# Branch stages of a hybrid decoder step: head norms, pooling, gathers and sample slots rearranged

## What is computed

```python
def _layer(x, ...):
    z = _rmsnorm(x, g1) @ w_in      # q k v | pooling input | mLSTM q k v, gates, output gate | 3 branch gates
    q, k = head-wise _rmsnorm(q), _rmsnorm(k)
    ya = sliding-window attention, window 128, 8 heads of 64, relative bias, sink per head
    yb = (trailing mean over 2/4/8/16 tokens, on four groups of 128 channels, minus the token) @ w_pool * pool_scale
    h  = mLSTM in chunks of 128 tokens (4 heads of 128), state C, n, m carried from chunk to chunk
    yc = head-wise _rmsnorm(h) * sigmoid(co)
    x  = x + (sigmoid(ga)*(ya@w_a) + sigmoid(gb)*(yb@w_b) + sigmoid(gc)*(yc@w_c)) @ w_out
    return x + _peer(_rmsnorm(x, g2))

def _peer(x):                       # for each token, 8 heads
    q = x @ wq; s1, s2 = q's halves @ 128 keys each
    top 16 of s1, top 16 of s2, top 16 of the 256 sums -> 16 experts of 16384, gates = softmax
    act = gelu(x . u[expert])
    y   = sum over 8*16 experts of gate * act * v[expert]
```

## Time and profile before

| | |
|---|---|
| median of 3 runs | 3914.45 us (3912.28 to 3915.92) |
| profiled execution | 3923.08 us, span 3921.3 us |
| TensorE matmul busy | 3242.6 us (83%) |
| VectorE busy | 2233.8 us (57%) |
| ScalarE busy | 1116.5 us (28%) |
| GpSimd busy | 1256.5 us (32%) |
| granted TensorE clock | 0.920 of 2.4 GHz over the span |
| DMA | 1317.12 MB, 336 GB/s; gathers 1082.20 MB |

### The profile page before, as it was taken

The page is one execution under the profiler, slowest core; times in us unless marked ns, Lnnn a source line. Parts: engine busy times, 40 slices in busy tenths (PEclk is TensorE's granted clock), DMA queues, the critical chain, the costliest instruction groups (busy, mean ns, idle before and its releaser), DMA issues. The chain is left out here.

```text
span 3921.3 us, 32232 instructions
## 1 busy us (share of the span) xinstructions
PE 3242.6 (83%) x10262; PEld 1874.4 (48%) x10262; DVE 2233.8 (57%) x5139; ACT 1116.5 (28%) x3364; POOL 1256.5 (32%) x1148
## 2 busy tenths in 40 slices
PE   7788879879989799669979799674699898778777
PEld 4577544446656444346656444342366563332222
DVE  0421577674556767664648665473545487764444
ACT  1211233342223323432223322342212233332222
POOL 0100233333433344343334333341233234443342
PEclk9789889989999899789999899886899999997999
DMA  5134899789999999679999898587899799999998
GB/s 161 58 100 144 331 366 395 292 329 363 420 397 389 378 408 421 244 297 415 420 392 406 350 353 334 220 339 231 318 373 389 264 404 411 421 420 265 421 421 372
DMA packets 204992, 1317.12 MB, mean 336 GB/s; under 512 B 23320, under 2 KB 27464, under 8 KB 72175
## 3 DMA queue, kind: packets, MB, share of 16 engines
q0 software_dynamic: 148736, 1082.20, 69.3%
q1 hardware_dynamic: 52631, 220.29, 15.0%
q10 hardware_dynamic: 3456, 12.58, 0.8%
HBM read 1298.67 MB, written 17.64 MB: 336 GB/s over the span
## 5 line engine op out<-in xcount | busy, mean ns | idle before, releaser
L1859 POOL DMA_INDIRECT arena<-uv,eidx x1040 | 1175.4, 1130 | 2358.8 <-PE ps L876 1797.1
L876 PE MATMUL ps<-arena,dgs 128*128 128x512 f32 x3508 | 1668.8, 620 | 255.1 <-ACT dgs L1178 253.8
L1410 DVE CUSTOM_DVE_ANT_0 arena<-arena,xx 128x1024 f32<-128x1024 f32 x1024 | 1236.9, 1224 | 695.9 <-DMA arena<-uv,eidx 671.4
L876 PEld LDWEIGHTS ps<-arena,dgs 128*128 128x128 f32 x3508 | 670.9, 198 | 1089.5 <-issue 698.6
L1159 ACT ACTIVATE gel<-dots 128x2 f32<-128x2 f32 (+1 forms) x520 | 105.0, 202 | 1643.4 <-DVE dots L1410 1642.3
L909 PE MATMUL ps<-wbuf,xT 128*128 128x420 f32 (+1 forms) x1152 | 428.2, 522 | 8.9 <-DMA wbuf<-w_z 7.7
L1057 PE MATMUL ps<-xT,wbuf 128*128 128x256 f32 (+1 forms) x1536 | 357.9, 387 | 5.8 <-DMA wbuf<-w_merge 3.7
L1057 PEld LDWEIGHTS ps<-xT,wbuf 128*128 128x128 f32 x1536 | 295.7, 193 | 75.1 <-issue 19.4
L1178 ACT ACTIVATE dgs<-cst,wgt 128x128 f32<-128x128 f32 x877 | 312.3, 395 | 16.7
L909 PEld LDWEIGHTS ps<-wbuf,xT 128*128 128x128 f32 (+1 forms) x1152 | 205.2, 180 | 232.0 <-issue 222.0
L1630 DVE SCALAR_TENSOR_TENSOR T<-T,ps 128x256 f32<-128x256 f32 (+1 forms) x96 | 40.6, 423 | 412.2 <-PE ps L1061 412.2
(11 more groups left out here) (353 smaller groups left out, 2087.6 us busy)
## 6 DMA issues: line engine op xcount, KB each, us to landing
wbuf<-w_merge SPq DMA_DIRECT2D x96, 768.0 KB, 8.5
wbuf<-w_z SPq DMA_DIRECT2D x64, 840.0 KB, 8.2
wbuf<-w_q SPq DMA_DIRECT2D x64, 512.0 KB, 8.0
arena<-uv,eidx POOLq DMA_INDIRECT x1040, 11.6
wbuf<-w_o SPq DMA_DIRECT2D x32, 512.0 KB, 7.8
xin<-x_prompt SPq DMA_DIRECT2D x8, 1024.0 KB, 8.5
grow<-gains SPq DMA_DIRECT2D x8, 512.0 KB, 9.5
xin<-biasfull SPq DMA_DIRECT2D x4, 1024.0 KB, 4.7
```

The lines of the kernel that those rows point to most:

```text
L876: done = mm(ps[:, half, :], dgs[:, j, :], ring[:, j, row_], start=(q == 0), stop=(q == P - 1), skip_group_check=True)
L1410: v.tensor_tensor_reduce(ring[0:rows_, j, 0:D], ring[0:rows_, j, 0:D], x, 1.0, 0.0, ALU.mult, ALU.add, dots[0:rows_, j:j + 1]).then_inc(s[ ...
L1859: g.indirect_dma_start(ring[0:rows_, j, :], None, uv, bass.IndirectOffsetOnAxis(ap=experts, axis=0)).then_inc(got[j], 16)
```

## The change

- **Head norms.** `head_norms` and `head_scales` run on VectorE in the projection, at chunks 5 and 11; ScalarE's square root, exponential and logarithm at chunk 8, the output gate's sigmoid at chunk 13. ScalarE's copies of q, k and of the pooling and mLSTM inputs are gone; the transposes read `z`.
- **Pooling** is a product with a band matrix on TensorE (four of 128x128 a tile, four of 16 columns for the rows of the tile before), copied by ScalarE to `pooled`. `pinT`, `tab` and `pool_tile` are gone; the table of constants that stays on the chip grows from 592 to 1168 columns.
- **GpSimd** issues gathers only, with no bound but the free ring buffers. The keys are shifted by VectorE; values and pooling rows of the tile before are read from `z` or, once a pass, from a copy by ScalarE.
- **Attention.** VectorE divides the softmax numerators before they are transposed, in two halves; the product with V is four matmuls of 512 columns, and gives the transposed result directly.
- **Norm of h**: squares, sums and the products with gate and gain are taken per tile, the rest jointly at the end.
- **Slots on VectorE.** In the last projection residues 1, 3, 5, 7 in place of 3: 171 slots in all.
- **Sample loads.** `sample_early` issues the stores and small loads in the branches of the last pass, behind `L0_ready` of its second tile; keys and values are loaded straight from the caches, only the last row of the keys from k_s. VectorE's order in the sample stage changes: mLSTM gates first, q and k norm after, pooling last.
- **Sample slots**: 8 of 128 rows (SPK = 8, slots 896 to 903). Experts 8 to 15 of each head are copied to partitions 64 to 127.
- **Start.** x is loaded before the constants; the spread of the bias table waits nowhere ahead of the first weights, and the bias load stands at weight chunk 8.
- VectorE ends a tile's sum one point later; the second weight load of a merge no longer waits for the pooling.

```diff
-SLOTS = TILES * P + PK
+SPK = PK // 2
+SLOTS = TILES * P + SPK
-ON_VECTOR = {"z": (3,), "b": (1, 5), "m": (1, 4, 6), "o": (1, 3, 5), "f": (2,)}
+ON_VECTOR = {"z": (3,), (LAST, "z"): (1, 3, 5, 7), "b": (1, 5), "m": (1, 4, 6), "o": (1, 3, 5), "f": (2,)}
...
@@ SyncE, the last pass
+        def sample_early(sp, at):
+            sp.dma_start(scr_qk, zs_scr[:, CQ0:CQ0 + 1024]...); sp.dma_start(scr_g..., zs_scr[:, G0:G0 + 8]...)
+            sp.dma_start(k_s[:, 0:W - 1, :], cache_k[:, 1:W, :]); ... v_s, pool_s likewise, selT, sel
+            sp.wait_ge(s["c_scr"], 32)
+            sp.wait_ge(s["tile_v"], tile.at("L0_ready", TILES))
+            g32, q32, k32, n32, c1, misc, relrep, sbuck loaded
         def sample_loads(sp, at):
             sp.dma_start(zs, zs_scr)
             sp.dma_start(spool[0:NS * HIST, :], state_pool...)
+            sp.dma_start(Ks[0:W - 1, :, :], cache_k[:, 1:W, :]...)
             load_c(0)
+            load_qk(0)
+            sp.dma_start(Vs[0:W - 1, :, :], cache_v[:, 1:W, :]...); sp.dma_start(Vs[W - 1:W, :, :], zs_scr[:, V0:V0 + P]...)
-            sp.wait_ge(s["kscr"], 64)
-            sp.dma_start(Ks, k_s.rearrange("n k c -> k n c")).then_inc(s["k_load"], 16)
-            sp.dma_start(Vs, v_s.rearrange("n k c -> k n c")).then_inc(s["k_load"], 16)
+            sp.dma_start(Ks[W - 1:W, :, :], k_s[:, W - 1:W, :]...)
...
@@ TensorE, branches
-                    pe.wait_ge(s["qks_ready"], here)
+                    pe.wait_ge(s["qkn"], p + 1)
-                        tr(ps[:, 2, j * P:(j + 1) * P], qks[:, j * P:(j + 1) * P], ident)
+                        tr(ps[:, 2, j * P:(j + 1) * P], z[:, t, j * P:(j + 1) * P], ident)
-                    for j in range(4):
-                        last = tr(ps[:, 6, j * P:(j + 1) * P], pcs[:, j * P:(j + 1) * P], ident)
+                    for c in range(4):
+                            mm(ps[:, 6, cols_], own, band[:, c, :], start=True, stop=False, skip_group_check=True)
+                            last = mm(ps[:, 6, c * P:c * P + 16], rows_, prev_band[64:P, c, :], start=False, stop=True, ...)
-                    pe.wait_ge(s["P_exp"], here)
                     for half in range(2):
+                        pe.wait_ge(s["P_normed" if half else "Pa_normed"], here)
-                    for h in range(AH):
-                        mm(ps[:, 2, o:o + AD], PT[:, 2 * h, :], vprev[:, 64 * kv:64 * kv + 64], start=True, stop=False)
-                        last = mm(ps[:, 2, o:o + AD], PT[:, 2 * h + 1, :], z[:, t, V0 + 64 * kv:...], start=False, stop=True)
+                    for kv in range(AKV):
+                        mm(out, z[:, 0, V0...] if t else vprev[...], PT[:, heads, :][:, 0::2, :], start=True, stop=False)
+                        last = mm(out, z[:, t, V0...], PT[:, heads, :][:, 1::2, :], start=False, stop=True)
-                    for j in range(4):
-                        last = tr(ps[:, 2, j * P:(j + 1) * P], qks[:, j * P:(j + 1) * P], ident)
-                    last.then_inc(s["yaT_tr"], 1)
...
@@ VectorE, projection and branches
+                    if c == 5:
+                        head_norms(p)
+                    if c == 11:
+                        head_scales(p)
+                    v.tensor_copy(kTr[:, 0:P], kTr[:, P:2 * P]).then_inc(s["tile_v"], tile.step("k_moved"))
+                    v.tensor_tensor(L[:, 0:AG, :], L[:, 0:AG, :], arden[:, 0:AG]..., ALU.mult).then_inc(s["Pa_normed"], 1)
+                    v.tensor_tensor(L[:, AG:AH, :], L[:, AG:AH, :], arden[:, AG:AH]..., ALU.mult).then_inc(s["P_normed"], 1)
...
@@ GpSimd
-            for p in range(PASSES):
-                for t in range(NT):
-                    ahead(p, "b", t, 0)
-                    pool_tile(p, t)
-                    ahead(p, "b", t, 3)
-                    shift_keys(p, t)
-                    ahead(p, "b", t, 6)
-                    shift_values(p, t)
             gather(SLOTS)
```

More of the change, by code:

```diff
@@ L609, in sample_vector @@
             v.scalar_tensor_tensor(n32, n32, c1[:, 19:20], t32, ALU.mult, ALU.add).then_inc(s["smp_v"], SMP["v"].step("c_nn2"))
+            point(LAST, "x", 1)
+            dve.wait_ge(s["r40"], n)
+            zq = zs[:, 0:640].rearrange("p (h d) -> p h d", d=AD)
+            v.tensor_tensor(zq, zq, r40[0:NS, 0:10].unsqueeze(2).broadcast_to([NS, 10, AD]), ALU.mult).then_inc(s["smp_v"], SMP["v"].step("q_qk_scaled"))
+            dve.wait_ge(s["smp_v"], SMP["v"].at("q_qk_scaled"))
+            v.tensor_tensor(zs[:, 0:640], zs[:, 0:640], row[0:NS, R_QK:R_QK + 640], ALU.mult).then_inc(s["qkn"], 1)
+            point(LAST, "x", 2)
+            dve.wait_ge(s["smp_a"], SMP["a"].at("b_T"))
+            for c, w in enumerate(POOLW):
+                last = v.tensor_reduce(psum_s[:, c, :], full[:, c, :, 16 - w:16], AX.X, ALU.add)
+            last.then_inc(s["smp_v"], SMP["v"].step("b_s1"))
+            dve.wait_ge(s["smp_v"], SMP["v"].at("b_s1"))
+            for c, w in enumerate(POOLW):
+                last = v.scalar_tensor_tensor(pool_s_in[:, c, :], psum_s[:, c, :], 1.0 / w, full[:, c, :, HIST], ALU.mult, ALU.subtract)
+            last.then_inc(s["smp_v"], SMP["v"].step("b_p"))
+            point(LAST, "x", 3)
             dve.wait_ge(s["smp_p"], SMP["p"].at("a_qtr"))
@@ L754, in _, with weights @@
             used = [None]
-            def weights(src, shape, count, sem, base, per, between=(), free_after=None):
+            def weights(src, shape, count, sem, base, per, between=(), later=None):
                 width = int(np.prod(shape))
@@ L771, in weights @@
                 for i in range(2, count):
+                    if i == 8 and later:
+                        later()
                     sp.wait_ge(sem, base + per * (i - 1))
@@ L828, in _ @@
                 tiles = len(tiles_of(p))
-                weights(w_z, (HALF, ZP), NZ, s["z_mm"], NZ * tiles_before(p), tiles, [lambda: load_bias(p)])
+                weights(w_z, (HALF, ZP), NZ, s["z_mm"], NZ * tiles_before(p), tiles, [lambda: load_bias(p)] if p else [spread_bias], None if p else lambda: load_bias(p))
                 if p == LAST:
@@ L877, in add_slots @@
                         else:
-                            done = mm(ps[0:NS, 4 + half, :], dgs[0:PH * NS, j, 0:NS], ring[0:PH * NS, j, row_],
-                                      start=(q == 0), stop=(q == PK - 1), skip_group_check=True)
+                            done = mm(ps[0:NS, 4 + half, :], dgs[:, j, 0:NS], ring[:, j, row_],
+                                      start=(q == 0), stop=(q == SPK - 1), skip_group_check=True)
                     done.then_inc(free[j], 1)
@@ L1398, in point @@
                 first, last = PLAN[p].get(key, (0, 0))
+                if first == last:
+                    return
+                if ended[0] < TILES - 1 and passed[0] > last_of(ended[0]):
+                    end_tile(ended[0])
+                passed[0] = first
                 for n in range(first, last):
@@ L1415, in point @@
                         unadded.append(n)
-                if ended[0] < TILES - 1 and first > last_of(ended[0]):
-                    end_tile(ended[0])
             def norm(p, which):
@@ L1906 @@
         C[bucket[W - 1 - i], C_SBUCK + i] = 1.0
[L1907 to L1911 removed]
+    selmat = np.zeros((P, NS + P), f)
+    for i in range(P):
+        selmat[i, i % NS] = 1.0
+        selmat[i % NS, NS + i] = 1.0
     perm = np.array([kv * AG + j for j in range(AG) for kv in range(AKV)])
```

459 lines of the change are left out of this document (214 added, 245 removed).

## The result

The changed kernel takes 3828.15 us (median of 4 runs, 3815.5 to 3835.04) against 3913.36 before: ratio 0.9778, 95% interval 0.9757 to 0.9799. It is faster, by 85 us in the medians and by 97.7 in the profiled executions (3825.35 us against 3923.08), and outside my range, which ended at 3820.

The account below looks back on a forecast made before the run. No engine was full: the branches were taken as a chain of short steps, DMA as the floor where slots run freely. Terms -5 + 4 - 88 - 28 - 27 - 36 = -180 from 3923.08, scaled by 0.9978, gave 3735 us; 8-in-10 range 3660 to 3820.

Parts of the forecast that it names:

- Sample loads early and without the round trip of keys and values: Sample stage: TensorE's 19.5 us wait goes, and some two thirds of an 11.7 us load wait; -27 us.
- Head norms: Head of the branches: TensorE's 47.2 us wait before the first transpose goes, -47; table loads in projections 1 and 2, +4.
- Pooling from GpSimd: Branches: gathers no longer queue behind GpSimd's pooling; 15 us in each of passes 2 and 3, 4 in pass 1, -34.
- Softmax normalised before the transposes: Branches: second normalisation lies on the chain, transposes of the attention output go; +0.4 us a tile, +3 in all.
- h norms per tile: End of the branches: squares of both tiles leave the path to ycT; -2.5 us a pass, -10.
- Projection 3: Last projection: 24 more slots on VectorE shorten the stage from 237.9 to 210 us; -28, bounds -41 to -12.
- Sample slots of 128 rows: Tail: half the instructions for the same bytes; the 36 us of DMA time lost in a 90 us hole go, -36.
- The smaller sum beside it: Tail: if 64-row gathers were not narrow and only TensorE was late, 40 - 27 = 13 us instead of 36.
- Rival B: Branches held by ring buffers TensorE frees late and dots in order, so the stall is not GpSimd's; 3823 us, chance 0.19.
- the 20 to 40 that I gave as a sign of being right: Branches 2 and 3: dots' waits for gathers at 20 to 40 us in place of 52 and 48.
- C, the pace of DMA: Branches fall to DMA's pace, 121 us against 179.5 and 179.8; 3648 us, chance 0.19.
- D: Merges and projections: weights land late as gathers share the DMA engines, so the kernel is slower; 4051 us, chance 0.05.

Follow-up runs that it names:

- Experiment 12: Changed kernel with 127-row loads cut into 112 and 15 and the branches' end reordered, head norms, gates and sigmoid back at the head of the branches: 3799.18 us, ratio 0.9702.
- experiment 4: Kernel before the change without GpSimd's ten pooling operations and its wait for the transposed pooling input, pooled part left out: 3883.79 us, ratio 0.9917.
- experiment 6: Changed kernel with 127-row loads cut into 112 and 15, almost all of the pooling's band products left out: 3765.4 us, ratio 0.9612.
- experiment 7: Changed kernel with 127-row loads cut into 112 and 15, without the two products that divide the softmax numerators: 3771.31 us, ratio 0.9623.
- experiment 5: Changed kernel with 127-row loads cut into 112 and 15, joint h norm and yc copy moved before the last point's dots: 3760.3 us, ratio 0.9603.
- experiment 10: Changed kernel with 127-row loads cut, branches' end reordered, pooling products moved, plus per-tile h norm behind the copy of the softmax transposes' second half: 3745.09 us, ratio 0.9565.
- experiment 3: Changed kernel with 127-row loads cut into 112 and 15, last projection's VectorE slots back to one residue of 8 in place of four: 3823.44 us.
- experiments 1 and 2: Changed kernel with 127-row key and value loads cut into 112 and 15: 3790.1 us; with the round trip back, 128-row loads from k_s and v_s: 3788.41 us.
- experiment 8: Changed kernel with 127-row loads cut into 112 and 15, the tail's last 120 slots gathering only 64 of 128 rows: 3794.2 us, ratio 0.968.

## Why the prediction was wrong

The direction was right and most steps too; the step that failed is *Sample loads early and without the round trip of keys and values*, and behind it two costs put at nothing or almost.

- *Head norms* (-47 and +4): right. Experiment 12 has 39 us for the 43.
- *Pooling from GpSimd*: the -34 was right in size (30 by experiment 4), its working only in part: the dots' waits for gathers fell by 12 us in branches 2 and 3, not by 30, and the slower operations of VectorE, which the sum had at nothing, are in the 30 too. "On TensorE four products of 128x128 a tile come in for four transposes and half a softmax transposition that leave: nothing" was wrong: the products cost 25 us (experiment 6), less what the transposes had cost. I had left out the four of 16 columns beside them, each with a weight load of its own, and I took TensorE's idle share for room. The net of the pooling's move is some 5 us and what the transposes had cost.
- *Softmax normalised before the transposes* (+3): 19 to 22 (experiment 7), less what left with the old division. I had one of two scalings beside other work; here both cost about their length.
- *h norms per tile* (-10): the joint part stayed behind six dots and two row adds, TensorE's wait grew from 6.1 to 11.3 us, and 30 us were left lying (experiment 5), 14 more in the order of the per-tile part, probably (experiment 10).
- *Projection 3* (-28): -40 in the profile, 33 in the medians (experiment 3). VectorE's row adds did not hold up the dots as I had feared (VectorE is busy 168.66 us); the bound of 194 from DMA was nearly reached, 197.7.
- *Sample loads* (-27): the step that failed, +33 for the stage. With the loads cut the stage and branches 3 are 31 us shorter than before, the stage alone some 14. The wait of 19.5 us that I let go with the round trip did not go: TensorE waits 21.6 us without the round trip and 20.9 with it (experiments 1 and 2). The number of rows was in the diff, 127 in place of 128, and I priced the loads by bytes and by the trip that went.
- *Sample slots of 128 rows* (-36): right, -33, and by the cause weighed there, not by TensorE alone (experiment 8). The 32 matmuls last 20 us at 421 GB/s, and the hole is gone. The smaller sum beside it, 40 - 27 = 13, set twelve of the sixteen slots against all eight; the sixteen took 48 us, which makes it 21.

Rival B named 3823 us, near what came, but not for its reason: the pooling on GpSimd cost 30 us (experiment 4) and projection 3's gain stayed (experiment 3). Its picture of the branches was half right: the dots still wait for gathers, 42.0 and 38.4 us in branches 2 and 3 of the changed kernel, at the upper end of the 20 to 40 that I gave as a sign of being right. C, the pace of DMA, needs branches of 121 us; 164 came, and 140 with fewer slots. D did not happen: weights land in 8.4 us, and TensorE's waits for them are no longer than before:

```profile
wbuf<-w_merge SPq DMA_DIRECT2D x96, 768.0 KB, 8.4
```

By the experiments' sizes the forecast's -180 becomes about -180 + 38 (loads) + 25 (pooling products) + 16 (scaling) - 7 (projection 3) + 4 (pooling on GpSimd) + 4 (heads) + 3 (tail) = -97, against -97.7. That it comes out so close is luck, as each is known to some 17 us, the 25 and the 16 are without what left in exchange, and the 12 us that the sample stage still lacks with its loads cut (-15 for the -27, if branches 3 have their -16) and the missing -10 at the end of the branches are not in it. What those two are set off against stays open, as does why a slot more costs the projections only 1.1 us.

## What to carry to other kernels

A stage that no engine fills can be a chain. In this one, work moved into it cost about its length on TensorE and on VectorE, though neither was full, and work moved out of it paid; so first ask whether the filler work put into such a stage is cheaper elsewhere. Where a loop's last small step decides what comes next, try it ahead of the filler on every engine (30 us here). Price a transfer by its shape, not by its bytes alone: one row fewer than 128 cost 38 us here, and half the rows of a gather saved nothing.

## What the runs showed of the hardware

- A load of 127 rows of 8 x 512 bytes to SBUF held the next issue of the same queue for 55.52 us, and one like it for 29.55; as 112 + 15 rows the issue behind the keys took 0.40 us. While the loads of 127 rows were under way and nothing else was, the core moved 20 GB/s.
- An indirect gather of 64 rows of 8 KB to partitions 0 to 63 lasts as long as one of 128 rows: 68 gathers in 180 us both times, 207 against 412 GB/s, DMA share 1.02 against 0.99.
- Beside the pooling on GpSimd a row add of VectorE took 2.15 us; with the pooling left out none took over 1.31, and VectorE was busy 12.8 us less over the kernel.
